# GpSimd instead of VectorE subtracts the rounded part of the compression's ten weight units

## The reference

```
tb = t[:, :, blk_idx] + cmp_pe[j]
h = jax.nn.silu(tb.reshape(B, G, n_cmp, CMP_BLOCK * hd) @ cmp_w1[j])
return h @ cmp_w2[j]
```

## Time and profile before

| | |
|---|---|
| runs | 1647.71 us median of three (1645.72 to 1648.44) |
| profiled execution | 1646.79 us, its span 1645.0 us |
| TensorE busy | 1555.8 us, 95% of the span |
| VectorE busy | 859.8 us, 52% |
| ScalarE busy | 716.6 us, 44% |
| GpSimd busy | 405.2 us, 25% |
| mean granted clock of TensorE | 0.979 |

### The profile page before, as it was taken

The page is one execution under the profiler, slowest core; times in us unless marked ns, Lnnn a source line. Parts: engine busy times, 40 slices in busy tenths (PEclk is TensorE's granted clock), DMA queues, the critical chain, the costliest instruction groups (busy, mean ns, idle before and its releaser), DMA issues.

```text
span 1645.0 us, 23213 instructions
## 1 busy us (share of the span) xinstructions
PE 1555.8 (95%) x7566; PEld 1279.3 (78%) x7566; DVE 859.8 (52%) x1360; ACT 716.6 (44%) x1315; POOL 405.2 (25%) x436
## 2 busy tenths in 40 slices
PE   6999999898999999999999999999989999999996
PEld 4878777777778888888887777777768788888885
DVE  5764654665644343434566565555556434444345
ACT  5753665764432222222475446666533322222233
POOL 0301556665001010101011035756620101011010
PEclk9999999999999999999999999999999999999998
DMA  4233221114323222222323412111242232323232
GB/s 182 99 124 129 60 71 59 39 65 136 121 79 101 99 94 101 94 98 90 103 87 126 142 58 78 59 57 40 84 141 98 88 103 90 102 89 102 89 102 103
DMA packets 43526, 155.55 MB, mean 95 GB/s; under 512 B 5312, under 2 KB 5312, under 8 KB 43424
## 3 DMA queue, kind: packets, MB, share of 16 engines
q1 hardware_dynamic: 37440, 134.23, 24.6%
q0 software_dynamic: 5408, 17.95, 3.0%
q10 hardware_dynamic: 576, 2.10, 0.3%
HBM read 143.78 MB, written 10.49 MB: 94 GB/s over the span
## 4 chain that ended last, share of the span: by engine, by line
PE 74%; issue 13%; DVE 5%; POOL 4%; ACT 3%; DMA 1%; POOLq 0%; DVEq 0%; ACTq 0%
PE G L1307 12%; PE G L1309 12%; PE G L1308 12%; PE O L1307 7%; PE O L1309 7%; PE O L1308 7%; PE O L1573 3%; PE T L1549 3%; PE S L1532 2%; PE T L1307 1%; POOL wsplit L462 1%; PE T L1309 1%; PE T L1308 1%; POOL F L457 1%; ACT F L584 1%
## 5 line engine op out<-in xcount | busy, mean ns | idle before, releaser
L548 ACT ACTIVATE wsplit<-stage 128x1024 fp32r<-128x1024 f32 x230 | 242.0, 1052 | 275.1 <-PE G L1309 122.6
L869 DVE TENSOR_TENSOR wsplit<-stage,wsplit 128x1024 fp32r<-128x1024 f32 x192 | 238.6, 1243 | 52.7 <-ACT wsplit L548 52.6
L1307 PE MATMUL G<-xg,wsplit 128*128 128x512 f32 x592 | 245.7, 415 | 15.4 <-DVE xg L873 13.4
L1309 PE MATMUL G<-xg,wsplit 128*128 128x512 f32 x592 | 234.4, 396 | 0.0
L1308 PE MATMUL G<-xg,wsplit 128*128 128x512 f32 x592 | 233.8, 395 | 0.0
L541 POOL TENSOR_TENSOR F<-Y 128x512 f32<-128x512 f32 x64 | 66.7, 1042 | 669.1 <-DVE Y L1278 669.1
L705 ACT ACTIVATE F<-S,nmx 128x512 f32<-128x512 f32 x192 | 101.4, 528 | 153.8 <-DVE nmx L1081 152.9
L1081 DVE TENSOR_REDUCE nmx<-S 128x1 f32<-128x512 f32 x192 | 93.4, 487 | 123.1 <-PE S L1540 121.7
L849 ACT ACTIVATE area<-Y 128x512 fp32r<-128x512 f32 x64 | 40.5, 632 | 249.1 <-DVE Y L1278 249.1
L1307 PEld LDWEIGHTS G<-xg,wsplit 128*128 128x128 f32 x592 | 113.4, 191 | 38.8 <-DVE xg L873 16.4
L1309 PEld LDWEIGHTS G<-xg,wsplit 128*128 128x128 f32 x592 | 112.7, 190 | 24.9
(11 more groups left out here) (248 smaller groups left out, 3150.4 us busy)
## 6 DMA issues: line engine op xcount, KB each, us to landing
stage<-units SPq DMA_DIRECT2D x230, 512.0 KB, 3.3
stage_n<-units_n SPq DMA_DIRECT2D x22, 512.0 KB, 3.3
gates<-Y POOLq DMA_DIRECT2D x32, 256.0 KB, 2.8
E<-gates POOLq DMA_DIRECT2D x16, 256.0 KB, 3.7
F<-gates POOLq DMA_DIRECT2D x16, 256.0 KB, 3.9
x<-x_in ACTq DMA_DIRECT2D x4, 512.0 KB, 11.4
out<-F SPq DMA_DIRECT2D x6, 256.0 KB, 2.1
rope<-tables POOLq DMA_DIRECT2D x1, 768.0 KB, 9.9
```

The lines of the kernel that those rows point to most:

```text
L548: act.activation(wslot(u)[:, 0, :], staged(u), ACT.Copy).then_inc(s_whin if u in SN else s_whi, 1)
L869: dve.tensor_tensor(wslot(u)[:, 1, :], staged(u), wslot(u)[:, 0, :], ALU.subtract)\
L1307: pe.matmul(dst, a(0), b(0), start=first, stop=False)
L1309: return pe.matmul(dst, a(1), b(0), start=False, stop=last)
```

## The change

In `PREFIX` of both layers the ten subtractions for the narrow units leave VectorE and go to GpSimd, in the order of `SMALL`. The operation and its operands are the same. They are queued behind the two `key_rest` calls, and GpSimd waits first until its own key rests have landed. Behind the units n = 6, 7, 8 and 9 it issues the stores of the gates 0, 1, 2 and 3, and then that of gate 4. Each subtraction is followed, behind the next one, by a wait for its completion.

```
@@ -462,6 +462,13 @@
+                def split_narrow(n):
+                    split_rounded(pool, l, SMALL[n])
+                    if n >= 1:
+                        split_done(pool, l, SMALL[n - 1])
+                    pool.tensor_tensor(wslot(SMALL[n])[:, 1, :], staged(SMALL[n]), wslot(SMALL[n])[:, 0, :], ALU.subtract)\
+                        .then_inc(s_wlon[n % 2], 1)
+
@@ -499,8 +506,14 @@
                 for br in range(2):
                     key_rest(br)
-                for i in range(FIRST_GATE):
-                    store_gate(i)
+                pool.wait_ge(s_kl, l * 2 + 2)
+                for n in range(NS):
+                    split_narrow(n)
+                    for i in range(FIRST_GATE):
+                        if SMALL_AT.get(("GATE", i)) == [n]:
+                            store_gate(i)
+                store_gate(FIRST_GATE - 1)
+                split_done(pool, l, SMALL[NS - 1])
@@ -1205,8 +1218,6 @@
                     if item in (("GATE", 3), ("GATE", 4)):
                         compressed_max(i - 3)
-                    for n in SMALL_AT.get(item, []):
-                        split_lo(l, SMALL[n])
```

## The result

The changed kernel takes 1652.76 us (median of five, 1651.29 to 1655.75) against 1647.71 before (five runs, 1645.72 to 1648.44). The ratio is 1.0041, with a 95% interval of 1.0027 to 1.0056: slower. The two medians alone differ by 5.05 us, a ratio of 1.0031; the ratio on record stands for about 6.8 us, and its interval, 4.4 to 9.2 us, holds both. The profiled execution has a span of 1650.3 us, 5.3 more than that of before.

The account below looks back on a forecast made before the run. TensorE, busy for 95% of the span, was taken as the bound. 2 x 1.09 + 2 x 1.10 + 0.69 + 1.6 = 6.7 us on 1646.79 gave 1653.5, put at 1654.0 towards the median; range 1650.8 to 1658.5.

Parts of the forecast that it names:

- n = 0 and n = 5: Narrow units TensorE waits for in each layer: GpSimd's slower subtraction makes it start 1.09 and 1.10 us later, twice each.
- The exclusion and the 0.14: GpSimd and VectorE both reading SBUF: the second waits for the other's end, then needs its own duration less 0.14 us.
- `csq`: VectorE's product behind n = 3: held by GpSimd's subtraction, TensorE starts 0.69 us later in layer 1, nothing in layer 0.
- The clock: TensorE behind the longer wait for n = 5 in layer 0: one more drop to the lower clock, 1.6 us.
- a sign of being wrong: Over the whole kernel: the prediction is wrong if TensorE's clock drops change by more than one.
- the third rival: GpSimd's subtractions hold VectorE's big-unit subtractions or query rests until TensorE waits, or two or three new clock drops; 1658, chance 0.19.
- The terms as a sum: Later TensorE starts at n = 0, n = 5 and `csq` plus one clock drop: 6.7 us more than the profiled execution.
- What costs nothing: The other sixteen units end 1.1 us or so later, hidden behind TensorE's other products; later loads and stores cost nothing.
- n = 7, the closest: The narrow unit with least cover among those said to cost nothing: GpSimd done 0.97 us before TensorE comes.
- The other side: Faster: longer waits shift work against TensorE's clock, seven drops of 1.6 us go, 4.5 faster, 1642.3; chance 0.04.

Follow-up runs that it names:

- the doubled kernel: The full change with GpSimd's subtractions of n = 0 and n = 5 each done twice in a row; 1672.05 us in the profiled execution.

## Why the prediction was right

The forecast was slower by 5.1 to 6.7 us, at 1654.0 in a range of 1650.8 to 1658.5. Measured were 1652.76, and 5.3 us in the spans.

- *n = 0 and n = 5.* I had the waits at 1.8, 1.8, 3.2 and 3.4; they are 1.81, 1.81, 3.42 and 3.41. Four waits grew by 4.6 us together, against 4.4 in the sum. That these units are the cost is shown by the pair of the two halves, 1.0045 with them alone and 1.0006 with the other eight.
- *The exclusion and the 0.14.* GpSimd ends 2.24 after VectorE's rotation (predicted 2.23), VectorE's `csq` 1.15 after GpSimd (predicted 1.15). At n = 0 and n = 5 the exclusion adds little, 0.13, since VectorE's rotation was nearly over; at n = 3 it turned a gain of up to 0.54 us into a loss of 0.7, as the run with n = 3 alone shows.
- *`csq`.* The mechanism was right, its term of 0.69 was not paid in this execution: the stretch ahead of it ran at the lower clock and hid it. In the kernels where that clock stayed up the wait is 1.25 (n = 3 alone; 1.3 with the other eight and with the two earlier roundings on GpSimd), where 1.23 was computed. In the full change the 0.54 of before went too, so the term was -0.54 here.
- *The clock.* One more drop was forecast, 1.6 us, behind n = 5 in layer 0. It came, and so did two others in the first parts; two later ones went. Net this is about one drop, and that the net fits is luck: three drops are new and two are gone, where the prediction allowed one and named more than one as a sign of being wrong. Two or three new drops were a condition of the third rival, and for the first parts alone that came true. Where drops fall further on can't be read from a trace of before.
- *The terms as a sum.* 4.6 - 0.5 + 1.7 is 5.8, and layer 0 reached n = 0 0.76 us sooner in this execution, ahead of anything changed (ScalarE's rounding at 75.17 against 75.93). That gives 5.0 against the 5.3 of the spans. The sum of 6.7 was 1.4 too high: `csq` by 1.2 and the earlier start by 0.8, against 0.3 that the waits and the clock were sized too low and 0.3 that the terms leave over.
- *What costs nothing.* n = 7, the closest, shows no wait, and no big unit, load or store became what TensorE waits for. The third rival's collisions on the path have fallen for this kernel, though the doubled kernel shows its kind: 0.9 us more at each n = 0 once GpSimd stays on longer. The other side, seven drops going, did not come; single drops do come and go among executions.

## What to carry to other kernels

Moving an instruction to an idle but slower engine is priced by its lead over its consumer, not by busy time: here 16 of 20 moved instructions cost nothing that can be told, and the four without a lead carry the 5 us. Look first for how to give those a lead; with three roundings earlier in ScalarE's queue and `csq` earlier in VectorE's, the medians were 5.3 us (GpSimd) and 7.5 us (VectorE) below the kernel before, and the engines 2.2 apart, where they were 5 apart in the old order and 4.5 with only two roundings moved. The Trainium skill's "GPSIMD Engine Reference", section "When to use GPSIMD", sends elementwise work to VectorE because GpSimd takes about twice the time; 2.40 against 1.22 us agrees, and yet it decides only where no lead is left. And when a wait goes, look at what is late next: n = 6 had been hidden by n = 5.

## What the runs showed of the hardware that was not expected

The lower clock behind a wait was not tied to its length in a simple way. Behind waits of 1.8 to 3.4 us it was at half for 3.4 us or, as in the kernel with n = 0 and n = 5 alone, not at all; around waits of 5.1 to 5.8 us it was at half for 6.6 to 6.7 us each time, four of four. That execution had 11.4 us more of waiting and 19.9 us more of span, but some 5 us of this belong to a stretch at half clock that lies 200 us behind. Where the drops of a run fall also differed with the instants: in the changed kernel, 8 us late, two of them were gone over 200 us behind the last moved subtraction. One drop costs 1.7 us, within the spread among executions of one kernel, some 5 us, and a gain or loss of one drop should not be read as an effect.
